# A hybrid decoder step: a scan in two levels, outputs woven with gate blocks, and the first expert head on unnormalised h

## What is computed

```python
n = rmsnorm(h, norm1_g); z = n @ w_in + b_in          # u_s5 512 | conv 2*512 | q 512 | gates 3*1024
bu = einsum('gnc,btgc->btgn', b_bar, u)                # 32 groups, 64 complex states each
_, states = lax.associative_scan(lambda e1, e2: (e2[0]*e1[0], e2[0]*e1[1] + e2[1]), (a, bu), axis=1)
y = einsum('gcn,btgn->btgc', c_mat, states).real + d * u
zz = gelu(y); br_s5 = (zz * sigmoid(zz @ glu_w + glu_b)) @ w_s5_proj
br_conv = silu(layernorm(causal_depthwise_conv_31(a))) @ w_conv_proj
br_xa = softmax(q @ k.T / sqrt(128)) @ v @ w_xa_proj   # 256 memory tokens, 4 heads
h = h + (sigmoid(g0)*br_s5 + sigmoid(g1)*br_conv + sigmoid(g2)*br_xa) @ w_out
x = rmsnorm(h, norm2_g); q = x @ w_q                   # PEER: 8 heads, 2 x 128 keys
experts, gate = top16(top16(q1 @ keys1.T) + top16(q2 @ keys2.T))
h = h + sum_k gate_k * gelu(u[experts_k] . x) * v[experts_k]
y = rmsnorm(h, final_norm_g)
```

## Time and profile before

| | us |
|---|---|
| median of 3 runs | 1997.32 (1997.23 to 1998.0) |
| profiled execution, its own time | 1994.91 |
| its span, first to last instruction | 1993.3 |
| TensorE busy | 1714.8 (86%) |
| VectorE busy | 1384.0 (69%) |
| POOL busy | 662.2 (33%) |
| ScalarE busy | 515.7 (26%) |
| first gather issued | 500.10 |

### The profile page before, as it was taken

The page is one execution under the profiler, slowest core; times in us unless marked ns, Lnnn a source line. Parts: engine busy times, 40 slices in busy tenths (PEclk is TensorE's granted clock), DMA queues, the critical chain, the costliest instruction groups (busy, mean ns, idle before and its releaser), DMA issues.

```text
span 1993.3 us, 18438 instructions
## 1 busy us (share of the span) xinstructions
PE 1714.8 (86%) x5539; PEld 1021.0 (51%) x5539; DVE 1384.0 (69%) x3580; ACT 515.7 (26%) x1208; POOL 662.2 (33%) x604
## 2 busy tenths in 40 slices
PE   8999698999999999979789998777787877777777
PEld 7888686888655555546345553333233312333332
DVE  5986766233777777776887667777767777777755
ACT  3121132402223333331222332223122212222211
POOL 1120110000334444434443444443443444444342
PEclk9989879999999999989899998999988998999988
DMA  5452543453999999989999999999999999999996
GB/s 207 135 85 74 158 102 106 147 167 103 398 418 418 418 418 418 416 360 395 401 413 420 417 393 421 421 422 422 422 397 422 417 422 414 414 413 421 413 409 289
DMA packets 112110, 674.09 MB, mean 338 GB/s; under 512 B 12720, under 2 KB 15104, under 8 KB 42000
## 3 DMA queue, kind: packets, MB, share of 16 engines
q0 software_dynamic: 80816, 577.23, 71.6%
q1 hardware_dynamic: 30640, 94.82, 13.8%
q10 hardware_dynamic: 560, 0.92, 0.2%
HBM read 665.79 MB, written 6.21 MB: 337 GB/s over the span
## 4 chain that ended last, share of the span: by engine, by line
PE 43%; DMA 36%; issue 8%; DVE 8%; POOL 2%; ACT 2%; DVEq 0%; ACTq 0%; POOLq 0%
DMA upper<-in_peer_uv,upper 22%; PE pair L985 20%; DMA lower<-in_peer_uv,upper 13%; PE pair L611 6%; PE pair L906 5%; PE pair L600 5%; POOL upper L576 1%; ACT upper L1322 1%; DVE upper L1501 1%; DVE upper L1532 1%; DVE upper L1539 1%; DVE upper L1756 1%; DVE upper L1537 1%; POOL lower L576 1%; PE pair L652 1%
## 5 line engine op out<-in xcount | busy, mean ns | idle before, releaser
L985 PE MATMUL pair<-upper 128*128 128x512 f32 (+1 forms) x1184 | 582.9, 635 | 133.7 <-ACT upper L1322 133.7
L576 POOL DMA_INDIRECT upper<-in_peer_uv,upper x324 | 369.9, 1142 | 496.5 <-PE pair L985 428.1
L985 PE MATMUL pair<-lower,upper 128*128 128x512 f32 (+1 forms) x792 | 391.6, 637 | 88.3 <-ACT upper L1322 88.3
L985 PEld LDWEIGHTS pair<-upper 128*128 128x128 f32 (+1 forms) x1184 | 225.3, 197 | 429.1 <-issue 273.1
L576 POOL DMA_INDIRECT lower<-in_peer_uv,upper x220 | 252.8, 1149 | 516.8 <-PE pair L985 306.7
L985 PEld LDWEIGHTS pair<-lower,upper 128*128 128x128 f32 (+1 forms) x792 | 151.5, 198 | 287.8 <-issue 192.2
L1756 DVE CUSTOM_DVE_ANT_0 upper<-upper 128x1024 f32<-128x1024 f32 x172 | 210.6, 1225 | 120.8 <-DMA upper<-in_peer_uv,upper 120.6
L1756 DVE CUSTOM_DVE_ANT_0 upper<-upper,lower 128x1024 f32<-128x1024 f32 x152 | 185.9, 1223 | 93.4 <-DMA upper<-in_peer_uv,upper 92.8
L1322 ACT ACTIVATE upper<-upper 128x128 f32<-128x128 f32 (+1 forms) x494 | 164.7, 386 | 302.4 <-DVE upper L1771 302.2
L1756 DVE CUSTOM_DVE_ANT_0 lower<-lower,upper 128x1024 f32<-128x1024 f32 x116 | 142.1, 1225 | 88.6 <-DMA lower<-in_peer_uv,upper 88.4
L1202 ACT ACTIVATE upper<-upper 128x4 f32<-128x4 f32 x136 | 27.9, 205 | 634.2 <-DVE upper L1756 634.1
(11 more groups left out here) (341 smaller groups left out, 1716.6 us busy)
## 6 DMA issues: line engine op xcount, KB each, us to landing
lower<-in_w_in SPq DMA_DIRECT2D x64, 512.0 KB, 6.0
lower<-in_peer_q SPq DMA_DIRECT2D x32, 512.0 KB, 7.9
lower<-in_proj SPq DMA_DIRECT2D x48, 256.0 KB, 6.9
lower<-in_w_out SPq DMA_DIRECT2D x16, 512.0 KB, 5.7
upper<-in_peer_uv,upper POOLq DMA_INDIRECT x324, 11.6
upper<-in_cache_k SPq DMA_DIRECT2D x8, 512.0 KB, 4.5
upper<-in_cache_v SPq DMA_DIRECT2D x8, 512.0 KB, 4.5
lower<-in_peer_uv,upper POOLq DMA_INDIRECT x220, 11.5
```

The costliest lines, as they stand in the source:

```text
L576: pool.indirect_dma_start(row(g), None, a["peer_uv"], bass.IndirectOffsetOnAxis(ap=idx[:, n % 8, j:j + 1], axis=0)).then_inc(row_in[g % RI ...
L985: mm = pe.matmul(pairs[n % 2][0:rows, h, :], diag[:, (nth - 1) % DIAGS, 0:rows], row(g)[:, D + h * 512:D + (h + 1) * 512], start=(j == min ...
```

## The change

The scan becomes two-level. Seven steps run inside all eight blocks of eight chunks at once (512 columns an operation, elements eight words apart), seven steps carry the block ends (64 columns), and the carries, times powers of the chunk factor, are added to the real states inside the blocks (784 columns). The powers are worked out on VectorE ahead of the convolution.

```diff
             link(dve.memset(Z[:, :, :, NB:NB + 1], 0.0))
-            with dve.Fori(0, NC // L) as i:
-                for r in range(L):
...
+            parts = Z[:, :, :, NB + 1:].rearrange("p e g (s r) -> p e g s r", r=8)
+            for r in range(1, 8):
+                src, dst = parts[:, :, :, :, r - 1], parts[:, :, :, :, r]
+                tt(st0, src, A8.unsqueeze(3).to_broadcast([P, 2, G, 8]), ALU.mult)
+                for e in range(2):
+                    ins = tt(st1[:, e], src[:, 1 - e], B8[:, e, :].unsqueeze(2).to_broadcast([P, G, 8]), ALU.mult)
+                link(ins)
+                link(tt(st0, st0, st1, ALU.add))
+                link(tt(dst, dst, st0, ALU.add))
+            for s in range(1, 8):
...
+            for h in range(2):
...
+                    ins = tt(ct, carry, power, ALU.mult)
+                link(ins)
+                link(tt(ct0, ct0, ct1, ALU.add))
+                link(tt(dst, dst, ct0, ALU.add))
```

```diff
+            def woven(small, large, skip=0):
+
+                for i, _ in enumerate(small):
+                    if i >= skip:
+                        next(large, None)
+                for _ in large:
+                    pass
+
             scores(0)
-            gates(2, 4)
             pe.wait_ge(scan_ok, 1)
...
+            woven(out_of_states(0, 0, 14), gate_by_gate(2, 4))
+            woven(out_of_states(1, 14, 28), gate_by_gate(4, 6), 8)
+            woven(out_of_states(2, 28, 32), gate_by_gate(6, 7))
             turn(0)
             scores(1)
-            gates(4, 5)
+            gates(7, 8)
...
-            gates(11, 13)
+            gates(13, 15)
+            woven(sample_values(), gate_by_gate(15, 17))
             ps = begin("ss_x")
             emptied(pe, "ss_o")
```

```diff
             for j in range(8):
                 first(f"o{j}", merged, KD, merged_ok if j == 0 else None, KD)
-            ps = begin("ss2")
...
+                if j == 5:
+                    square_columns(0, 4)
+                    first_head(0, 4)
+                if j == 6:
+                    square_columns(4, 6)
+                    first_head(4, 6)
+            square_columns(6, 8)
+            first_head(6, 8)
...
-                    act.activation(sc(h)[:, b, :], ps[:, 0:P], ACT.Copy)
+                    act.activation(sc(h)[:, b, :], ps[:, 0:P], ACT.Copy, scale=rcol[:, 0:1])
...
-            for k in range(KD):
-                stt(xbT[:, k, :], h2T[:, k, :], c("g2", k), h2r, ALU.mult, ALU.mult).then_inc(xbT_ok, 1)
+                ts(xbT[:, j, :], h2T[:, j, :], c("g2", j), None, ALU.mult).then_inc(xbT_ok, 1)
+            dve.wait_ge(square_sums, 1)
```

More of the change, by code:

```diff
@@ L776, in _ @@
             values(1)
-            gates(6, 7)
+            gates(9, 10)
             turn(2)
@@ L1201, in gelu_of, with first_head @@
                 act.wait_ge(u_used, GROUP * k + GROUP)
-                act.activation(gel[:, n % 2, j:j + GROUP], dots[:, n % 2, j:j + GROUP], ACT.Gelu).then_inc(gel_ok, 1)
+                t = EXPERTS[n][0]
+                act.activation(gel[:, n % 2, j:j + GROUP], dots[:, n % 2, j:j + GROUP], ACT.Gelu,
+                               scale=rcol[:, t:t + 1] if t < 2 else 1.0).then_inc(gel_ok, 1)
+            def first_head():
+                for b in range(2):
+                    act.wait_ge(first_q, b + 1)
+                    act.activation(qbuf[:, 0, b, 0:FIRST], pairs[b][:, 1, 0:FIRST], ACT.Copy).then_inc(first_q_out, 1)
+                act.wait_ge(rcol_ok, 1)
+                act.activation(rcol, rcol, ACT.Sqrt).then_inc(rcol_ok, 1)
+                act.wait_ge(rcol_ok, 3)
             def first_query(h):
```

298 lines of the change are left out of this document (182 added, 116 removed).

## The result

| | before | changed |
|---|---|---|
| median of 5 runs, us | 1997.32 | 1986.13 (1985.68 to 1989.41) |
| profiled execution, its own time | 1994.91 | 1986.13 |
| its span | 1993.3 | 1984.5 |
| first gather | 500.10 | 487.52 |
| eleventh gather | 527.52 | 519.33 |

The ratio is 0.9946, with an interval of 0.9933 to 0.9959: 10.8 us (8.2 to 13.4) shorter. The direction is as forecast, the size is not half of it, and the time lies outside the range. The forecast's first gather was 472, 15.5 us too early; that is the error to explain.

The account below looks back on a forecast made before the run. It took TensorE as the bound before 500 us, then full DMA engines. Terms gave minus 28.2 for the first gather, minus 24.2 for the eleventh; that and 0.6 for small things, from 1997.32, made 1972.5 us (1963.5 to 1984), chance 0.62.

Parts of the forecast that it names:

- Scan, minus 13.5: VectorE's scan falls from 80.8 to 46.6 us, so TensorE's wait of 13.5 us for it goes.
- The collision, plus 3: POOL's output transfers, released earlier by the scan, meet SP's last key loads: plus 3 us, bounds 0 and 9.
- Rival A: All five key loads collide with POOL's output transfers: plus 9 instead of 3, 1978.5 us; chance 0.15.
- Outputs woven, minus 12.9, plus 1.1, plus 2.9: TensorE's 128 output passes take 14.5 instead of 27.4 us; two new waits on VectorE's takeover add 1.1 and 2.9.
- rival D: TensorE's clock stays at 1.2 GHz through the woven stretch: slower, 2005 us; chance 0.04.
- Slow work behind the outputs: Softmax transposes and scores behind the outputs from states lose their slowness (0.87 and 1.48): minus 2.3 us.
- sample values, Gelu: Waits at cached values (2.0) and GLU (2.39) go, minus 4.4 us; wait for VectorE's sample sums, plus 1.2.
- first head: Reordered work between the last output block and first scores brings the first gather another 3.3 us forward.
- The low end of its range: No collision and the early first gather counted in full: minus 34, 1963.5 us.
- The end: DMA engines run dry for about 4 us before the eleventh gather, so the end follows it: minus 24.2 us.
- Rival B: The early first gather counts in full as VectorE catches up: minus 28.2, 1969 us; chance 0.12.
- C: Rival: operations with hops cost twice as much, the scan takes 78 us and TensorE still waits; 1991 us; chance 0.05.

Follow-up runs that it names:

- e3: Kernel before the change with only the two-level scan and its powers put in; 1996.8 us, ratio 1.0001.
- e1: Changed kernel with one wait added on POOL: its four output transfers start only after TensorE's first outputs from states; 1972.4 us, ratio 0.9888.
- e2: Changed kernel in which only the two large output transfers (mem_k, mem_v) wait for the first outputs from states; 1985.8 us, ratio 0.9958.
- e5: On e1, both products of each output read the same contiguous weights, leaving out the coupling inside a chunk; 1968.1 us, one run.
- f1: On e1, weaving undone: five gate blocks first, then the outputs from states alone; 1977.9 us, ratio 0.9903.
- f2: On e1, the first head put back as in the kernel before; 1975.8 us, ratio 0.9900.
- e8: On e1, gate blocks spread evenly, third part not woven, VectorE's taps moved to idle stretches, root's table loaded earlier; 1963.0 us, ratio 0.9819.
- e4: Changed kernel in which the first gather also waits for the second head's scores on TensorE; 1992.0 us, ratio 0.9983.
- f4: Changed kernel in which the eleventh gather waits for the third row used up by TensorE instead of the first; 1989.4 us, ratio 0.9965.

## Why the prediction was wrong

**Scan, minus 13.5: right.** 46.1 us against 46.6. Its cost of hops was taken from the earlier trace rows. By the worst figure of the Trainium skill (Vector Engine (DVE) Microarchitecture Reference, 5.2 Measured stream behaviour on trn2) it would have been 60 us, by my estimate; the measured 46.1 do not reach that. But e3 shows that without e1's wait the term is worth nothing.

**The collision, plus 3: the step that failed first.** It cost 14.2 in the scores (changed kernel against e1). I had seen that POOL's transfers would start at 206 and meet the key loads, and took the nearest row, a 512 KB load beside the gathers, 4.5 us longer, with 9 as the bound. Two things are wrong with that. The neighbour in the earlier trace rows moves 8 KB pieces at over 400 GB/s; the convolution's history moves in pieces of 120 bytes, at a share of 0.90 and 72 GB/s, which stood in the earlier trace rows, and e2 shows that it alone makes nine tenths of the cost, with a third of the bytes. And the bound counted the waits alone (10.6 measured, 9.3 more than before): the granted clock falls to 0.50 in the wait of 6.55, which costs another 4.6 us in the two key groups and the first scores. Rival A's price for the waits (9) was right nearly to the us, but by luck: its condition, a scan ended at 195 and all five loads hit, did not occur (202.6; the first two waits, 0.24 and 0.48, are no longer than before), and its 1978.5 also lacked the clock.

**Outputs woven, minus 12.9, plus 1.1, plus 2.9: the step that failed second.** From 218.30 to 266.24 the kernel before needed 47.9 with two gate blocks; the changed one needs 43.1 with five. Less three blocks (10.4) that is minus 15.2, of which 13.5 are the scan's wait; the outputs themselves gave 1.7 instead of 8.9 (12.9 less the two waits). I costed a pass at the 0.113 us of the 64 passes at 138.42, of equal shape. Half of the outputs' passes load weights in hops, at 303 ns instead of 192 (e5). The rows of the outputs before couldn't show it: there, at the 1.2 GHz level, both kinds took the same (326 and 324 ns). With contiguous weights the outputs come out at my rate (0.45 a pair) and the first takeover wait at my 1.1; with the hopped ones that wait is 0. The second wait is 2.64, forecast 2.9. The clock, which I held at 2.4 GHz throughout, fell twice, in the run of 21 bare products and behind that wait (247 to 254 and 268 to 271 us). By the rates of the same rows at 1.00 this cost some 2.6 and 1.6 us. The hops, by the two rates of e5, cost some 4.5 (0.20 on each of 12.5 bare outputs, 0.10 on each of 19.5 woven ones), and the two waits were 1.4 less than forecast: together about the 7.2 that are missing. The reason that the prediction gives for the low clock before, the idle stretch ahead, is not needed for it: in f1 the clock falls in the bare products with nothing idle ahead. Its argument against rival D, the 64 passes at 138.42 that kept the full rate, came from passes whose weights took 192 ns.

**Slow work behind the outputs, sample values, Gelu, first head: minus 2.3, minus 4.4, plus 1.2, minus 3.3.** Together minus 8.8; measured minus 10.1 (from the first transposes to the first gather 233.9 before and 213.4 after, less the three gate blocks). The waits at the cached values and at the GLU are gone, the wait for the sample sums is 1.26. The first head is worth about 2 of it (f2).

**Sum.** Minus 28.2 was forecast for the first gather, minus 12.6 came: 11.1 lost in the scores, 7.2 in the outputs, 2.7 won in the rest and in an earlier start of the sample scores. All three signs that the prediction named for being wrong came: a first gather later than 480, full engines from it on, and a low clock in the woven stretch. The low end of its range does not follow from the items named for it: minus 28.2 without the collision of 3 is minus 31.2, not 34.

**The end.** I let it follow the eleventh gather, since the engines would run dry before it. The reason was wrong: from 1.5 to 3 us behind the first gather on the share is 1.0 in the changed kernel, in e1 and in e8. Besides the ten rows seven loads of query weights, 512 KB each, are issued by SP between the first and the eleventh gather. The share of 0.97 at 526, from which I read that the ten rows had just landed, shows no more than full engines. As a rule it did no harm. Over the ten timed kernels the shift of the eleventh gather meets the measured shift with an error of 2.2 us (root of the mean square), that of the first with 4.0. A count that needs no gather's time does nearly as well, 2.6: the bytes that all queues have moved by 600 us, over 418 GB/s. The summary line of all DMA traffic up to 600 us, before and then changed:

```profile
DMA packets 28069, 105.62 MB, mean 176 GB/s; under 512 B 3372, under 2 KB 5756, under 8 KB 23404
```

```profile
DMA packets 28846, 110.10 MB, mean 184 GB/s; under 512 B 3443, under 2 KB 5827, under 8 KB 23728
```

4.48 MB more are 10.7 us, for 10.8 measured; e8, with 120.87 MB, 36.5 for 36.2; e2, with 111.50 MB, 14.1 where 8.4 (5.8 to 11.2) was measured. The bytes follow for the most part from the first gather, so the count is no independent cause. Whether the eleventh gather or the bytes set the end isn't settled by e4 and f4. Rival B's price for it, the first gather in full, is the worst of the three.

C and D didn't occur, though what D describes, the half clock in the outputs, did for 7 and 3 us.

## What to carry to other kernels

When a stall is removed, list what else waited for the same event and price that against what it will meet, by its kind of transfer and not by its bytes: here the transfers that the early scan released, a third of their bytes in short pieces, cost 14.2 us, more than the 13.5 that the scan gave. A wait on TensorE may cost more than its length: look at what runs behind it at half clock (4.6 us behind the wait of 6.55). And before a duration is carried over to a matmul of equal shape, see whether its weights lie in memory in the same way; here the low clock hid the difference.

## What the runs showed of the hardware

- Weights read in hops of 32 words load in 303 ns, contiguous ones of the same shape in 192 (changed kernel and e5). At the granted clock of 0.50 they took 326 and 324 (before).
- TensorE counts as busy and still loses the clock: in f1 it is busy without a gap from 218 to 260, and the clock is 1.00 in the gate blocks (to 235.59) and 0.50 in the bare products from 244 on. With contiguous weights a run of 21 bare products kept 1.00 (e5), in which with hops it fell (changed kernel, e1).
- While the convolution's history moved in runs of 120 bytes, the 16 DMA engines stood at a share of 0.9 to 1.2 with 60 to 170 GB/s. Of the five key loads beside it the median landed in 6.1 us and the slowest in 15.6, against 4.4 and 4.5 before. The Trainium skill (DMA: Bandwidth & Descriptors, Issuing engines are not separate DMA queues) says that transfers of SP and POOL run on the same 16 engines and interleave; the trace agrees, and gives the price.
